# Linear attention by levels: two wide levels in open banks, five narrow ones as 32x32 diagonal blocks

## What is computed

```python
def gla_chunked(q, k, v, log_a, s0):
    ...
    causal = jnp.tril(jnp.ones((GLA_CHUNK, GLA_CHUNK), dtype=bool))[:, :, None]

    def step(s, inp):
        qc, kc, vc, gc = inp
        b = jnp.cumsum(gc, axis=2)
        o_inter = jnp.einsum('bhcd,bhde->bhce', qc * jnp.exp(b), s)
        rel = jnp.where(causal, b[:, :, :, None, :] - b[:, :, None, :, :], -jnp.inf)
        att = jnp.sum(qc[:, :, :, None, :] * kc[:, :, None, :, :] * jnp.exp(rel), axis=-1)
        o_intra = jnp.einsum('bhij,bhje->bhie', att, vc)
        ...
    return o.transpose(1, 0, 3, 2, 4).reshape(B, T, H, dv), s_fin
...
ob_f, sg_f = gla_chunked(qb, kb, vb, lg_f, sg_f0)
ob_b, sg_b = gla_chunked(flip_t(qb), flip_t(kb), flip_t(vb), flip_t(lg_b), sg_b0)
o_b = (ob_f + flip_t(ob_b)).astype(x.dtype)
```

## Time and profile before

| | before |
|---|---|
| median of 3 runs | 2029.49 us (2025.91 to 2033.86) |
| span of the profiled execution | 2030.6 us |
| PE busy | 1819.7 us, 90% |
| DVE busy | 1036.8 us, 51% |
| ACT busy | 736.9 us, 36% |
| POOL busy | 148.0 us, 7% |
| DMA | 214.48 MB, mean 106 GB/s |
| mean granted clock of PE | 0.958 |

### The profile page before, as it was taken

How to read it: one execution, slowest core, us unless ns; L and a number is a source line. 1 busy time by engine, 2 the same in 40 slices (tenths; PEclk the granted TensorE clock), 3 DMA queues, 4 the chain that set the end, 5 groups by cost and what they waited for, 6 DMA issues and landing times.

```text
span 2030.6 us, 38851 instructions
## 1 busy us (share of the span) xinstructions
PE 1819.7 (90%) x16819; PEld 1537.5 (76%) x16819; DVE 1036.8 (51%) x1859; ACT 736.9 (36%) x1297; POOL 148.0 (7%) x325
## 2 busy tenths in 40 slices
PE   5799888868897999999989989888688889999998
PEld 3799555536765989999989975555466669899998
DVE  1536437887634463334342454497775446533332
ACT  2334435333343343333243434523332343433321
POOL 2000000033300000000000000000522000000000
PEclk8899999979898999999999999999899999999999
DMA  8444231111305445663443423311013154344342
GB/s 264 162 118 123 69 117 61 48 42 44 107 2 161 145 125 150 163 176 99 126 134 107 135 90 104 103 54 47 2 44 107 44 171 124 85 129 131 109 117 85
DMA packets 267936, 214.48 MB, mean 106 GB/s; under 512 B 7225, under 2 KB 259544, under 8 KB 267512
## 3 DMA queue, kind: packets, MB, share of 16 engines
q1 hardware_dynamic: 264816, 204.41, 33.3%
q0 software_dynamic: 2736, 7.54, 1.2%
q10 hardware_dynamic: 216, 0.06, 0.0%
HBM read 209.10 MB, written 2.88 MB: 104 GB/s over the span
## 4 chain that ended last, share of the span: by engine, by line
PE 73%; DVE 16%; ACT 5%; issue 4%; POOL 1%; DMA 1%; SPq 0%; ACTq 0%; DVEq 0%; POOLq 0%
PE bank L565 12%; PE bank L570 12%; PE bank L566 12%; PE bank L624 7%; PE bank L1181 3%; PE bank L1180 3%; PE bank L1179 3%; PE bank L990 3%; DVE gate L2076 3%; PE bank L630 2%; PE bank L621 2%; PE bank L524 1%; PE bank L999 1%; PE bank L603 1%; PE bank L932 1%
## 5 line engine op out<-in xcount | busy, mean ns | idle before, releaser
L566 PE MATMUL bank<-scr_rounded 128*128 128x384 f32 x1344 | 453.7, 338 | 0.0
L566 PEld LDWEIGHTS bank<-scr_rounded 128*128 128x128 f32 x1344 | 254.7, 190 | 1.3
L565 PE MATMUL bank<-scr_rounded,gate_rounded 128*128 128x384 f32 (+1 forms) x672 | 228.9, 341 | 11.8 <-ACT scr_rounded L1365 9.3
L565 PE MATMUL bank<-scr_rounded 128*128 128x384 f32 (+1 forms) x672 | 227.0, 338 | 13.6 <-ACT scr_rounded L1365 13.0
L624 PE MATMUL bank<-h,ring 128*128 128x384 f32 x576 | 213.3, 515 | 11.7 <-DVEq L351 8.3
L570 PE MATMUL bank<-scr_rounded,gate_rounded 128*128 128x384 f32 (+1 forms) x672 | 222.9, 338 | 0.0
L570 PE MATMUL bank<-scr_rounded 128*128 128x384 f32 (+1 forms) x672 | 222.0, 336 | 0.0
L1804 DVE TENSOR_TENSOR scr_rounded<-ring,gate_rounded 128x2048 fp32r<-128x2048 f32 (+3 forms) x65 | 135.4, 2083 | 157.9 <-ACT gate_rounded L1354 157.3
L1804 DVE TENSOR_TENSOR scr_rounded<-ring,scr_rounded 128x2048 fp32r<-128x2048 f32 (+1 forms) x65 | 135.4, 2083 | 136.9 <-ACT scr_rounded L1354 135.4
L624 PEld LDWEIGHTS bank<-h,ring 128*128 128x128 f32 x576 | 108.7, 198 | 91.0 <-issue 33.3
L1354 ACT ACTIVATE gate_rounded<-ring 128x2048 fp32r<-128x2048 f32 (+3 forms) x65 | 113.6, 1747 | 153.1 <-PE bank L570 67.9
(11 more groups left out here) (387 smaller groups left out, 3176.8 us busy)
## 6 DMA issues: line engine op xcount, KB each, us to landing
ring<-in_w_in_dram SPq DMA_DIRECT2D x56, 1024.0 KB, 5.4
ring<-in_w_ada_dram SPq DMA_DIRECT2D x48, 1024.0 KB, 5.3
ring<-in_w_ffn_in_dram SPq DMA_DIRECT2D x88, 512.0 KB, 5.3
ring<-in_w_ffn_out_dram SPq DMA_DIRECT2D x32, 704.0 KB, 4.6
ring<-in_w_out_dram SPq DMA_DIRECT2D x8, 1024.0 KB, 5.1
ring<-in_w_po_a_dram SPq DMA_DIRECT2D x4, 1024.0 KB, 6.6
ring<-in_w_po_b_dram SPq DMA_DIRECT2D x4, 1024.0 KB, 7.6
ring<-in_w_po_c_dram SPq DMA_DIRECT2D x4, 1024.0 KB, 9.8
```

The costliest lines, as they stand in the source:

```text
L565: pe.matmul(o, w_hi[:, k, :], right[0][k], start=k == 0, stop=False)
L566: pe.matmul(o, w_lo[:, k, :], right[0][k], start=False, stop=False)
```

## The change

- The masks become 32 wide: `near` holds, for the five narrow levels and both directions, which elements of a 32x32 block the level makes, and `eye32` the diagonal. The always needed constants move ahead of `dup`, so the reused part has 1504 columns of constants and the tile keeps its size.
- Wide levels (n = 0 to 3, w = 64 and 32): each makes only the rectangles that it needs, w rows by w columns, straight at their places in four banks (`far`), which stay open for all four steps. There is no masked copy. ACT empties the four banks into `att` (L1580 of the new kernel) in steps 4 and 5.
- Narrow levels (n = 4 to 13, w = 16 to 1): all their elements lie in the four 32x32 blocks on each chunk's diagonal. PE makes those blocks alone (`near_blocks`), 48 products of 32x32 (four heads, three chunks, four blocks), in two banks: partitions 32q to 32q+31 hold block q. DVE's masked copies are two of 128x192, into a tile `diag`. The first product `attd` is made in the same form.
- At the end `diag` is put at its places in `att`, over what the far banks left there: two of the four strips by DVE, two by ACT. PE waits for both before the product with the values.
- `zl[n % 2]` was protected by the waits for emptied banks; for the wide levels DVE now waits for a semaphore of PE (`gla_far`).

```diff
-        upper[k] = ((p[:, None] // (2 * h) == p[None, :] // (2 * h)) & (p[:, None] % (2 * h) < h)
-                    & (p[None, :] % (2 * h) >= h))
-    put("upper", upper.transpose(1, 0, 2).reshape(128, -1))
-    put("lower", upper.transpose(2, 0, 1).reshape(128, -1))
+        met = key // (2 * h) == query // (2 * h)
+        near[:, 0, k, :] = met & (key % (2 * h) < h) & (query % (2 * h) >= h)
+        near[:, 1, k, :] = met & (key % (2 * h) >= h) & (query % (2 * h) < h)
...
@@ -215,6 +222,7 @@
         sfin = take(512, 2, 2, 128)
         zz, lg = take(4 * T, 4, T), take(4 * T, 4, T)
         att = gate[:, 0:4, :]
+        diag = cst[:, NCONST:NCONST + T].rearrange("p (f b q) -> p f b q", f=2, b=2 * C)
         vbt = gate[:, 4:8, :].rearrange("p a b -> p (a b)").rearrange("p (c n) -> p c n", c=C)
...
@@ -464,6 +473,10 @@
 
             latent = (2 + s, 5 - s)[d]
             return [(s, 1 - s)[d], latent] if s < 2 else [latent]
+
+        def near_part(q):
+
+            return att[32 * q:32 * q + 32, :, :].rearrange("p a (c q) -> p (a c) q", c=C)[:, :, 32 * q:32 * q + 32]
 
         def state(d, c):
@@ -773,17 +786,22 @@
                         b = item("A", "z", l, 2 * d + hp)
                         pe.matmul(b[:, 0:T], lora[0:32, 0, 256 * d + 128 * hp:256 * d + 128 * hp + 128],
                                        pb[0:32, 12, :], start=True, stop=True).then_inc(psum_ready, 1)
-                for hp in range(2):
+                def near_blocks(kind, l, n, keys, queries):
+
                     pair = []
-                    for hh in (2 * hp, 2 * hp + 1):
+                    for f in range(2):
                         pe.wait_ge(*room())
-                        pair.append(item("V", "attd", l, hh))
-                    for cc in range(C):
-                        cs = slice(CH * cc, CH * cc + CH)
-                        for r, b in zip(hr, pair):
-                            ins = pe.matmul(b[:, cs], pb[r, 2 + hp, cs], pb[r, hp, cs], start=True, stop=True)
-                            if cc == C - 1:
-                                ins.then_inc(psum_ready, 1)
+                        pair.append(item("V", kind, l, n, f))
+                    for hp in range(2):
+                        for cc in range(C):
+                            for q in range(4):
+                                at = slice(CH * cc + 32 * q, CH * cc + 32 * q + 32)
+                                cols = slice(32 * (C * hp + cc), 32 * (C * hp + cc) + 32)
+                                for r, b in zip(hr, pair):
+                                    ins = pe.matmul(b[32 * q:32 * q + 32, cols], keys[r, hp, at], queries[r, hp, at], start=True, stop=True)
+                    ins.then_inc(psum_ready, 2)
+
+                near_blocks("attd", l, 0, pb[:, 2:4, :], pb[:, 0:2, :])
                 fill(4)
                 for hp in range(4):
@@ -816,29 +834,41 @@
                             ins = pe.matmul(b[hr[half], 128 * hp:128 * hp + 128], kht[:, m, 64 * hh:64 * hh + 64],
                                             vbt[:, cc, 128 * hh:128 * hh + 128], start=True, stop=True)
                     ins.then_inc(psum_ready, 1)
+                far = []
                 for n in range(2 * LEVELS):
                     fill(1)
                     pe.wait_ge(S["gla_z"], told("gla_z", l, n + 1))
+                    z = zl[n % 2]
+                    if n >= FAR:
+                        near_blocks("att", l, n, z, z)
+                        continue
+                    while len(far) < 4:
+                        pe.wait_ge(*room())
+                        far.append(item("A", "far", l, len(far)))
+                    finished.append(("level", l, n))
+                    k, d = LEVELS - 1 - n // 2, n % 2
+                    w = 1 << k
                     for hp in range(2):
-                        pair = []
-                        for hh in (2 * hp, 2 * hp + 1):
-                            pe.wait_ge(*room())
-                            pair.append(item("V", "att", l, n, hh))
-                        for cc in range(C):
-                            for r, b in zip(hr, pair):
-                                zc = zl[n % 2][r, hp, CH * cc:CH * cc + CH]
-                                ins = pe.matmul(b[:, CH * cc:CH * cc + CH], zc, zc, start=True, stop=True)
-                                if cc == C - 1:
-                                    ins.then_inc(psum_ready, 1)
+                        for at in range(0, T, 2 * w):
+                            lo, hi = slice(at, at + w), slice(at + w, at + 2 * w)
+                            keys, queries = (lo, hi) if d == 0 else (hi, lo)
+                            rows = slice(keys.start % CH, keys.start % CH + w)
+                            for f, r in enumerate(hr):
+                                ins = pe.matmul(far[2 * f + hp][rows, queries], z[r, hp, keys], z[r, hp, queries], start=True, stop=True)
+                    if n < FAR - 1:
+                        ins.then_inc(S["gla_far"], 1)
+                    else:
+                        ins.then_inc(psum_ready, 4)
                 pe.wait_ge(*emptied("kv", l, 3))
+                pe.wait_ge(S["gla_near_v"], told("gla_near_v", l, 1))
+                pe.wait_ge(S["gla_near_a"], told("gla_near_a", l, 1))
                 outs_b = []
                 for hh in range(4):
-                    pe.wait_ge(*emptied("att", l, 2 * LEVELS - 1, hh))
                     pe.wait_ge(*room())
                     outs_b.append(item("V", "ob", l, hh))
                     for cc in range(C):
                         cs = slice(CH * cc, CH * cc + CH)
-                        pe.matmul(outs_b[hh][:, cs], vbt[:, cc, 128 * hh:128 * hh + 128], att[:, hh, cs], start=cc == 0, stop=cc == 0,
+                        pe.matmul(outs_b[hh][:, cs], vbt[:, cc, 128 * hh:128 * hh + 128], att[:, 2 * (hh % 2) + hh // 2, cs], start=cc == 0, stop=cc == 0,
                                   skip_group_check=True)
                 for hp in range(2):
...
@@ -1217,7 +1247,7 @@
                 if n < C:
                     sp.dma_start(mg[:, :, :].rearrange("p a b -> p (a b)")[:, D * n:D * n + D], rows_of_x[n]).then_inc(x_in, 16)
                 if n == 12:
-                    sp.dma_start(cst[:, early:], const[:, early:]).then_inc(consts_rest, 16)
+                    sp.dma_start(cst[:, early:NCONST], const[:, early:]).then_inc(consts_rest, 16)
 
         @block.gpsimd
@@ -1541,7 +1571,20 @@
                 for n in range(2 * LEVELS):
                     act.wait_ge(S["gla_x"], told("gla_x", l, n + 1))
                     A(xl[n % 2], xl[n % 2], ACT.Exp, scale=1.0 / 16).then_inc(*tells("gla_xe"))
+                    if n < FAR:
+                        side_work("level", l, n)
+                        continue
+                    if n < FAR + 2:
+                        for a in (2 * (n - FAR), 2 * (n - FAR) + 1):
+                            act.wait_ge(psum_ready, filled("far", l, a))
+                            A(att[:, a, :], bank("far", l, a)[:, 0:T], ACT.Copy).then_inc(*empties("far", l, a))
                     side_work("att", l, n, 0)
+                act.wait_ge(*last())
+                for f in range(2):
+                    act.wait_ge(*emptied("att", l, 2 * LEVELS - 1, f))
+                for q in (2, 3):
+                    ins = A(near_part(q), diag[32 * q:32 * q + 32, :, :, :].rearrange("p f b q -> p (f b) q"), ACT.Copy)
+                    ins.then_inc(*(step() if q == 2 else tells("gla_near_a")))
                 for hh in range(4):
                     act.wait_ge(*emptied("ob", l, hh))
@@ -1981,11 +2024,15 @@
 
                 dve.wait_ge(*emptied("z", l, 3))
                 stt(out=lg, in0=zz, scalar=-1.0, in1=zz, op0=mult, op1=amax).then_inc(*tells("gla_abs"))
-                for hh in range(4):
-                    side_work("attd", l, hh)
-                    dve.wait_ge(psum_ready, filled("attd", l, hh))
-                    b = bank("attd", l, hh)
-                    stt(out=c3(att[:, hh, :]), in0=c3(b[:, 0:T]), scalar=2.0, in1=over(ident, C), op0=mult, op1=mult).then_inc(*empties("attd", l, hh))
+                def near_bank(*tag):
+
+                    return bank(*tag)[:, 0:T // 2].rearrange("p (b q) -> p b q", b=2 * C)
+
+                for f in range(2):
+                    side_work("attd", l, 0, f)
+                    dve.wait_ge(psum_ready, filled("attd", l, 0, f))
+                    stt(out=diag[:, f, :, :], in0=near_bank("attd", l, 0, f), scalar=2.0, in1=over(K("eye32"), 2 * C), op0=mult, op1=mult).then_inc(
+                        *empties("attd", l, 0, f))
                 side_work("kkms", l, 0)
                 dve.wait_ge(S["gla_log"], told("gla_log", l, 1))
@@ -2064,16 +2111,26 @@
                             if n:
                                 dve.wait_ge(*last())
                             distance(n + 1)
+                        if 2 <= n < FAR + 1:
```

(23 more changed lines are left out.)

33 lines of the change are left out of this document (20 added, 13 removed).

## The result

The changed kernel takes 2007.28 us (median of 4 runs, 2002.43 to 2010.43), the kernel before beside it 2031.67 us (4 runs, 2025.91 to 2034.25): ratio 0.9883, 95% interval 0.986 to 0.9906. The gain is 24.4 us where 38 were forecast, and the time lies just outside the range of 1984 to 2007. A second set of four runs of the same kernel gave 2006.68 us, 0.9862 (0.9829 to 0.9894); one of these four took 2640.41 us at a granted clock of 0.64 and is left out of the ratio, and the other three lie between 1999.06 and 2007.04.

The account below looks back on a forecast made before the run. The prediction took VectorE (DVE) to bound the level loop: 2 x 18.8 us gained there, less 2 x 0.7 at the loop's end, plus 1.8 at the start, 38.0 us off, gave 1992 us, range 1984 to 2007.

Parts of the forecast that it names:

- PE's side: Level loop: a narrow level costs PE 1.0 us, 2.5 with filler, against 2.68 of DVE, so DVE stays the bound.
- Masked copies: Narrow levels: copies of 192 elements take 0.375 us, a pair 0.65; eight steps lose 0.68 less wait, 10.7 us a layer gained.
- The wide levels: Levels 0 to 3, without masked copies: four steps lose 2.02 us each, 8.1 us a layer.
- The loads: Weight loads released by the fillers move along with them; DMA share in the loop 0.12, no cost counted.
- second rival: Small matmuls cost 25 to 30 ns each, by hindering strips or a floor: 2022 to 2033 us, chance 6%.
- ACT and `gla_far`: Levels 4 and 5: ACT's two far copies, about 0.5 us each, delay nothing; DVE's waits for `gla_far` are already met.
- The end of the loop: Last product to L841: 3.4 us instead of 2.73, a loss of 0.7 us a layer (0.3 to 1.2).
- The start: First product `attd`, block from 1.53 to 1.0 us: gains 0.5 us in layer 0 and 1.3 in layer 1.
- PE takes over: Rival for the loop: small matmuls cost 15 ns, a narrow level 3.2 us of PE; 2004 us, chance 14%.
- small price of 25 ns: The second rival's floor between matmul starts: a narrow level would take 4.15 us of PE; chance 6%.
- The clock falls in the loop: Rival: PE at 1.2 GHz in the level loop, 10 us more a layer, 2051 us; chance 5%.
- What would show it: Signs for right (2.7 us a level, PE busy over 90%) and wrong (DVE waiting for PE, levels of 3 us and more).

Follow-up runs that it names:

- blocks_64: Changed kernel with each narrow level's 48 products of 32x32 made as 24 of 64x64 (computes wrong values): 1997.28 us, ratio 0.9825 to the kernel before.
- late_loads: Changed kernel with SyncE's two 1 MB weight loads held back until the loop's last DVE copy is done: 1997.64 us, ratio 0.9837 to the kernel before.
- narrow_only: Changed kernel with the four wide levels made and copied through masks as in the kernel before: 2019.74 us, ratio 0.994 to the kernel before.
- double_blocks: Changed kernel with each block matmul of the ten narrow levels issued twice, same result: 2067.07 us, ratio 1.0178 to the kernel before.
- late_thin_fill: late_loads with the filler's matmuls cut from 384 to 16 columns in the last eight levels: 38.6 and 39.1 us in the loop.

## Why the prediction was wrong, point by point

**The step that failed** is "PE's side", in its conclusion "It costs nothing, but the cover is thin, 0.2 us a level". Its price of a block was good: 1.02 us measured for 1.0, that is (1.02 - 0.19)/95 = 8.7 ns an entry for the 8 that I took. What was left out is the supply of instructions, which is no term of any busy time. A level of before had 48 + 8 instructions of PE in 4.02 us, one of after has 192 + 8 in 2.68 us. It could have been read from the trace of before. In the stage of small matmuls behind its loop PE already stops inside runs of like matmuls (waits of PE, 460 to 700 us: us in all, times, longest; then a line of the timeline):

```profile
PE bank L990 <- issue: 10.4, 8, 3.7
...
475.69 0.52 PE L990 MATMUL bank<-scr 64*64 64x64 f32 x20 [1.37 <-issue]
```

From 469 to 481 us and from 505 to 517 us the packets of 256 instructions start 3.4 to 4.3 us apart there. At 3.7 us, 200 instructions take 2.9, more than 2.68. Missing in the loop are 11.2 us, and blocks_64 gives 10.4 of them back (41.3 and 41.2 to 36.1). late_loads splits these into 6.3 for portions held up by the loads, with the low clock that follows, and 4.1 for the rate of the portions.

**Masked copies.** Right: the group's mean is 367 ns for 375, a pair 0.63 us for 0.65. Where nothing holds PE up the levels take 2.00, 2.46, 2.67 and 3.14 us for 2.02, 2.57, 2.68 and 3.23. The 0.55 us that the text of the prediction adds for a merge is too much, 0.46 is measured; its sum does not use it.

**The wide levels.** Right: narrow_only measures 8.1 us a layer step by step for 8.1, and 7.6 and 8.6 over the loop.

**The loads.** "the weights' loads, released by them, move along; the DMA share in the loop is 0.12" was read as harmless. The mean hid that for some 5 us the transfer engines were busy by 90% and more, just when the instructions had to come.

**The size of a portion.** In the pages of the profile a packet of queue 8 is 16 KB, and 3840 instructions more brought 15 of them more. The Trainium skill, page "Runtime: NRT & Kernel Launch", section "Instruction fetch mechanics", states that an engine's instructions are refilled in blocks of 16 KiB, 256 instructions; the traces agree. The section also says that the fetching is hidden, because instructions issue more slowly than they are filled. Here it is not: up to 3.3 us stand still in the middle of a block. The floor of about 25 ns between the starts of matmuls, which the Trainium skill states on the page "TensorE: Matmul & The Clock Gate", section "Wait — 56ns, not 53.3ns?", and which stands in my second rival, does not hold for blocks spread over eight parts: 8.7 ns are measured. Each part is then used every 70 ns, so for a single part nothing here tests it.

**ACT and `gla_far`.** Right; ACT's two far copies take 0.87 us together and nobody waits. One small coupling I missed: at 371.25 a gate copy of ACT stood before exponential 12, and DVE waited 0.97 us for it, but only because PE was late with that gate.

**The end of the loop.** Forecast 3.4 us behind the last product. blocks_64, where PE is not held up, has 3.9: the pair of copies of ACT takes 1.06 us and not 0.7 to 0.8, and the outputs start 2.2 us after PE's last block. With late portions it is 4.6 (layer 0) and 5.9.

**The start.** Forecast 0.5 and 1.3 us, measured 0.3 and 0.2. The 2.93 us of `attd` in layer 1 were a matter of the clock and not of the block: in blocks_64 and double_blocks, this stage takes 33.1 us in layer 1, 0.3 less than layer 0 of before (granted clock 0.95 in blocks_64); in the first profile after it fell into the low clock again (0.86, as before) and took 35.9. I took a disturbed row for a price.

**The rivals.** "PE takes over" gave 2004 at 15 ns an entry. That is near the result by luck, and by the wrong mechanism: it asked for blocks over 1.3 us, and the undisturbed ones take 1.02. The small price of 25 ns and the slower clock throughout did not come. "The clock falls in the loop" was true in small, 0.92, as a consequence of the stall.

**What would show it.** "Levels of 3 us and more" with DVE waiting for PE was the sign that I named for wrong, and it came; I had not asked what else could make PE late.

## What to carry to other kernels

Count PE's instructions per microsecond, beside its busy time: where small matmuls and short waits meet, here above 256 instructions in some 3.7 us, the supply of the program becomes the bound, and busy shares of 80% on both engines with "issue" gaps inside a run of like matmuls are its mark. There the number of matmuls counts and not their size: half as many of twice the columns gained 5 us a layer (blocks_64), and a filler of 16 columns instead of 384 nothing (late_thin_fill). Large loads that are due soon but not now are best sent when no engine runs short of instructions: here two waits on SyncE gave 6.3 us of the loop back, while the gain in the whole time is not clear of the scatter.

## What the runs showed of the hardware

- Matmuls of 64x32x32 that alternate between eight parts of the array start 8.7 ns apart; those of 64x64x64 on four parts, 48 in 0.93 us, take nearly the same time in all.
- The instruction packets stay mostly 3.5 to 4 us apart even when PE has nothing else to wait for (double_blocks, thin filler), so hardly more than 256 instructions in that time are to be had in these stages. A packet is under way for 1.1 us of it, PE goes on 1.2 to 1.6 us after it has landed, and the next packet mostly starts 1.0 to 1.5 us after that, which adds up to the 3.5 to 4. Why it is not asked for earlier stays open.
- After gaps of 2.77, 2.94 and 3.31 us PE ran the next filler at half speed (2.93, 2.93 and 2.80 us instead of 1.56); the gaps of 1 us in late_loads had no such effect (granted clock in its loops 0.99 and 1.00). In late_thin_fill, with 16-column fillers and gaps of up to 1.7 us, it was 0.75.
- With the two loads under way a packet of instructions that was due after 3.5 to 4 us started only after 7.0 (after, 352.5 to 359.5) and 6.7 us (double_blocks), and then took no longer than others (0.99 and 1.05 us). Whether it waits inside the transfer engines or ahead of them was not tested apart. The landing times of the loads say nothing of it: 6.4 and 7.2 us in layer 0 of the changed kernel, 5.2 and 6.4 in its layer 1, where packets are delayed too.
